# The scan step of a hybrid decoder trunk: conv taps between the chained states, y's low part a step later, the next states' load behind the sample update

## The chip, the cores and the metric

One core of one Trainium2 chip runs the whole kernel. The metric is the device time of one execution in microseconds (us); the time before is the median of three runs.

## What is computed

One inference step of a 2-layer trunk over T = 336 tokens: 64 sample tokens (8 running sequences of 8 steps), 16 meta tokens and 256 prompt tokens. Each layer is a SwiGLU FFN, a mixer and a second FFN. The part of the mixer that the change touches is the Mamba-2 scan. Cut to what matters:

```python
xbc = silu(depthwise_causal_conv(concat([conv0, xbc]), conv_w, conv_b))   # CONV_K = 4 taps
xs, bm, cm = split(xbc)                       # 32 heads of 64 channels, 4 groups, 128 states
dt = softplus(dt_raw + dt_bias)
# ssd_scan, chunk by chunk
lmat = exp(where(causal, seg, -inf))
cb = einsum('bcign,bcjgn->bcijg', cc, bc)
y_intra = einsum('bcijgr,bcjgrp->bcigrp', cb * lmat, xdt)
cs = einsum('bcjgn,bcjgrp->bcgrpn', bc, xdt * decay_end)
final, prev = scan(lambda s, c: (s * decay + cs, s))          # chained states
y_inter = einsum('bcign,bcgrpn->bcigrp', cc, prev) * exp(acum)
y = y_intra + y_inter + d_skip * xs
y = rmsnorm(y * silu(z), ssd_norm)
ssd_out = y @ w_ssd_branch
```

The new states (`final`) of the prompt and of each sample sequence are outputs too.

## The kernel before

Channels lie on the 128 partitions, tokens along the free dimension. Every product of an activation with a weight is made in three matmuls, high part times high part, low times high, high times low (`unit`, L1012). A weight unit is 8 tiles of 128 x 128: SyncE loads it (`wraw`), ScalarE makes its high part (`whi`, L429), GpSimd its low part (`wlo`, L354), two units ahead of their use.

The scan of a layer has 16 steps, one for each 128 channels (2 heads), four steps to a group. On TensorE, ScalarE and GpSimd the first three groups are a hardware loop over groups with four steps written out in its body, and the last group is unrolled behind it; so it is on VectorE too. No scheduler orders anything: each engine runs its own program, in the order written, and semaphores join them. A wait holds up everything behind it on its engine.

Step t on **TensorE** (`ssd_step`, L1121): the xBC unit of tile t+1 into bank 1; the chunk states (L1135, into `kb[3]`); the intra products (L1143, into `kb[0]`); `log_l` of t+1; the z unit of tile t into bank 0, with the products of the sample states in between (L1157, into `kb[1]`); the inter-chunk products of the prompt (L1164, `y_full`); the sample update (L1173, `su_full`); then, behind a wait for `y_read`, the token-major transposes of tile t+1 (`x_token_major`, L1118), which overwrite `kb[0]`.

Step t on **VectorE** (`ssd_step`, L782): the whole conv of tile t+1 (L735 to L747: history, entry, four taps with a drain between any two); behind the chunk states and behind the store of the last step's states (`so_free`), a copy (L789) and the chaining of the states (L794, `p_done`); `times_l` of t+1 (L770); the z bank times 1/rms (L809); y: times its decay (L813), plus D times x (L815), plus the intra part (L817, `y_read`), times the gate (L820, `val_in`); `times_dt` of t+1 (L779, L780); the sample states plus their update (L828, `so_done`); last the sum of squares (L832) and the low part of y (L833, `b_done`), which reads the z bank once more. TensorE's next z unit waits for `b_done`.

Step t on **ScalarE** (`ssd_step`, L511): a weight split, the exponentials of L, the conv rows' store and the SiLU of the conv (`silu_xbc`, L495, L496); a second split; the SiLU of z (L521); behind `val_in` the high part of y (L523) and its square (L524); the load of the next sample states (L534, behind GpSimd's `st_dec`); `head_rows` (two activations, L501); and, behind `so_done`, the store of the new states (L531), whose landing raises `so_free`.

GpSimd decays the sample states into the output tile `so` (L391) behind `so_free` and the load. `so` is one tile: decay, chaining and sample adds of a step write it, and the store reads it.

Of the kernel before, what the change touches and what calls it, by code (L numbers as in the profile page):

```python
# [19 lines left out]
F32 = mybir.dt.float32  # L20
# [6 lines left out]
CONV_K, MAX_WIN = 4, 16  # L27
# [25 lines left out]
G_SSD = 6 * KD  # L53
# [95 lines left out]
def build(nc, x_in, wts, par_in, con_in, own_dram, cst_in, pst_in, ssm_in, y_out, ssm_out, conv_out, pool_out):  # L149
    with ExitStack() as ctx:  # L150
# [153 lines left out]
        p_done = sem("states_chained")  # L304
        y_full = sem("y_products_ready")
# [111 lines left out]
        def _(act):  # L417
# [93 lines left out]
            def ssd_step(L, t, q, rows, last):  # L511
# [9 lines left out]
                act.activation(zb, zb, ACT.Silu).then_inc(gate_done, 1)  # L521
                act.wait_ge(val_in, L * N_VAL + V_Y + t + 1)
                act.activation(bhi[:, t, :], zb, ACT.Copy, scale=par[:, L, bass.ds(G_SSD + t, 1)]).then_inc(hi_done, 1)  # L523
                act.activation(sq[:, 0, :], zb, ACT.Square).then_inc(sq_done, 1)  # L524
                if not last:
                    act.wait_ge(st_dec, L * KI + t + 1)
                    load_states(L, t + 1)
# [123 lines left out]
        def _(dve):  # L651
# [76 lines left out]
            def conv(L, c, m, bank, pair, side):  # L728
# [12 lines left out]
                dve.drain()  # L741
                n = CW - HIST
                cv = gb[bank][:, 0:n]
                dve.tensor_scalar(cv, xp[:, 0:n], pcol(L, G_CW + CONV_K * c), None, ALU.mult)
                for k in range(1, CONV_K):
                    dve.drain()
                    ins = dve.scalar_tensor_tensor(cv, xp[:, k:k + n], pcol(L, G_CW + CONV_K * c + k), cv, ALU.mult, ALU.add)  # L747
                ins.then_inc(cv_in, 1)
# [33 lines left out]
            def ssd_step(L, t, j, g, g_next, pair, last):  # L782
                kt, q = L * KI + t, j % 2
                if not last:
                    conv(L, 2 * N_GROUPS + t + 1, M0["ssd"] + 2 * t + 1, XS_BANK, pair, 1 - q)
# [5 lines left out]
                for c, dst in ((1, pst[:, 1, :]), (2, so[:, SEQS * P:SO])):  # L791
                    for h in range(2):
# [5 lines left out]
                ins.then_inc(p_done, 1)  # L798
                if j == TILES_PER_GROUP - 1 and not last:
                    group_b(g_next)  # L800
# [10 lines left out]
                dve.wait_ge(e_exp, kt + 1)  # L811
                dve.wait_ge(y_full, kt + 1)
                dve.tensor_tensor(yi, yi, eab[:, q, :], ALU.mult)  # L813
                dve.drain()
                dve.scalar_tensor_tensor(t_a[:, 0, :], xs[:, q, :], pcol(L, G_D + t), yi, ALU.mult, ALU.add)  # L815
                dve.drain()
                dve.tensor_tensor(t_a[:, 1, :], kb[0][:, 0:T], t_a[:, 0, :], ALU.add).then_inc(y_read, 1)  # L817
                dve.drain()
                dve.wait_ge(gate_done, L * N_GATE + KF + t + 1)
                dve.tensor_tensor(zb, zb, t_a[:, 1, :], ALU.mult).then_inc(val_in, 1)  # L820
                if not last:
                    times_dt(L, t + 1)

                dve.wait_ge(st_dec, kt + 1)
                dve.wait_ge(su_full, kt + 1)
                for b in range(2):
# [3 lines left out]
                dve.wait_ge(hi_done, L * N_HI + H_Y + t + 1)  # L830
                dve.wait_ge(sq_done, L * N_SQ + S_Y + t + 1)
                dve.tensor_tensor(acc[:, :], acc[:, :], sq[:, 0, :], ALU.add)  # L832
                dve.scalar_tensor_tensor(blo[:, t, :], zb, pcol(L, G_SSD + t), bhi[:, t, :].bitcast(F32),  # L833
                                         ALU.mult, ALU.subtract).then_inc(b_done, 1)
                dve.drain()

            for L in range(DEPTH):
# [81 lines left out]
                with dve.Fori(0, N_GROUPS - 1) as g:  # L919
                    for j in range(per):  # L920
                        ssd_step(L, per * g + j, j, g, g + (j + 1) // per, per // 2 * g + N_GROUPS + (j + 1) // 2, False)
                for j in range(per):
                    ssd_step(L, KI - per + j, j, N_GROUPS - 1, N_GROUPS - 1, (KI - per) // 2 + N_GROUPS + (j + 1) // 2, j == per - 1)
# [493 lines left out]
```

## Time and profile before

| | |
|---|---|
| median of 3 runs | 2165.03 us (2163.43 to 2165.84) |
| the profiled execution's own time | 2164.07 us |
| its span | 2162.3 us |
| TensorE busy (matmul) | 2008.5 us, 93% |
| VectorE busy | 966.3 us, 45% |
| ScalarE busy | 925.6 us, 43% |
| GpSimd busy | 1246.0 us, 58% |
| chain that ended last | TensorE 84%, VectorE 9% |

The two scans lie at about 353 to 592 us and 1412 to 1662 us of the span. Durations are read from the profiled execution. Its time is the span and 1.8 us around it, and it lies 1 us below the median. In the views, PE is TensorE, PEld its weight loads, DVE VectorE, ACT ScalarE, POOL GpSimd; ACTq is ScalarE's sequencer, where DMAs are issued. A row of the timeline with x3 gives the time from the first's start to the third's end. "[0.98 <-DVE t_a L817]" is idle time before the instruction and what ended it; "issue" is time in which the engine waited for nothing that the profile shows.

### The profile page before, as it was taken

Reading aid. Unit: us, or ns where it says so; the run is one execution under the profiler, and the core shown is the slowest. Engines: PE = TensorE matmul, PEld = TensorE weight load, DVE = VectorE, ACT = ScalarE, POOL = GpSimd, SP = SyncE. Lnnn points to the kernel's source line nnn. Section 1 sums busy time; section 2 is a strip of 40 time slices with the busy share of each in tenths; the row PEclk is TensorE's granted clock in tenths of the full one; section 3 lists DMA queues with packets and bytes.
Section 4 is the critical chain, followed back from the end, with each engine's and each line's share of the span. In section 5 each row is a group of like instructions: output and inputs, shape, how many; then the busy total and the mean of one; then the engine's idle time right before and its main releaser. Section 6 shows DMA issues by size and latency. Waiting matters only on the chain.

```text
span 2162.3 us, 39577 instructions
## 1 busy us (share of the span) xinstructions
PE 2008.5 (93%) x13486; PEld 1972.4 (91%) x13486; DVE 966.3 (45%) x2021; ACT 925.6 (43%) x1354; POOL 1246.0 (58%) x555
## 2 busy tenths in 40 slices
PE   6999978999999997999999998789998999899997
PEld 6999977889899997999889998788888999889997
DVE  3221177777645425221152212777776363352212
ACT  4343355555333434333343333455554234443332
POOL 5667743444366565666666666434444666666675
PEclk9999998999899999999999999999999999999998
DMA  4444422444344443444434444234344444434442
GB/s 162 145 142 155 156 80 91 153 141 151 125 153 145 145 138 97 141 141 155 146 99 144 151 154 138 80 102 152 131 152 143 134 147 136 138 101 141 145 156 103
DMA packets 86328, 292.28 MB, mean 135 GB/s; under 512 B 15728, under 2 KB 15728, under 8 KB 86256
## 3 DMA queue, kind: packets, MB, share of 16 engines
q1 hardware_dynamic: 68544, 249.13, 35.8%
q10 hardware_dynamic: 17712, 42.22, 5.6%
q8 instruction: 42, 0.69, 0.1%
q14 instruction: 30, 0.25, 0.0%
HBM read 269.29 MB, written 22.02 MB: 135 GB/s over the span
## 4 chain that ended last, share of the span: by engine, by line
PE 84%; DVE 9%; DVEq 2%; issue 2%; DMA 1%; ACT 1%; POOL 1%; ACTq 0%; SPq 0%
PE gb L1021 25%; PE gb L1025 23%; PE gb L1024 23%; PE kb L1157 1%; PE gb L1073 1%; DVE gb L747 1%; PE gb L1076 1%; PE gb L1077 1%; DVEq L701 1%; PE kb L1143 1%; PE kb L1135 1%; DVE t_a L696 1%; DVE t_a L815 1%; PE kb L1118 1%; PE kb L1164 1%
## 5 line engine op out<-in xcount | busy, mean ns | idle before, releaser
L354 POOL TENSOR_TENSOR wlo<-wraw,whi 128x1024 fp32r<-128x1024 f32 x474 | 1139.5, 2404 | 829.7 <-ACT whi L429 811.9
L1021 PE MATMUL gb<-ahi,whi 128*128 128x336 f32 x2256 | 745.6, 331 | 21.3 <-ACT bc L496 6.3
L1025 PE MATMUL gb<-ahi,wlo 128*128 128x336 f32 x2256 | 721.7, 320 | 0.0
L1024 PE MATMUL gb<-alo,whi 128*128 128x336 f32 x2256 | 720.6, 319 | 0.0
L429 ACT ACTIVATE whi<-wraw 128x1024 fp32r<-128x1024 f32 x474 | 494.7, 1052 | 183.7 <-PE gb L1021 122.6
L1021 PEld LDWEIGHTS gb<-ahi,whi 128*128 128x128 f32 x2256 | 431.3, 191 | 27.8 <-POOL wlo L354 11.0
L1024 PEld LDWEIGHTS gb<-alo,whi 128*128 128x128 f32 x2256 | 431.6, 191 | 0.0
L1025 PEld LDWEIGHTS gb<-ahi,wlo 128*128 128x128 f32 x2256 | 429.4, 190 | 0.0
L1021 PE MATMUL gb<-bhi,whi 128*128 128x336 f32 x1248 | 395.6, 317 | 4.4 <-DVE blo L975 4.4
L1024 PE MATMUL gb<-blo,whi 128*128 128x336 f32 x1248 | 393.6, 315 | 0.0
L1025 PE MATMUL gb<-bhi,wlo 128*128 128x336 f32 x1248 | 393.2, 315 | 0.0
L710 DVE TENSOR_TENSOR t_a<-gb,rpre 128x336 f32<-128x336 f32 x176 | 88.6, 507 | 341.1 <-PE gb L1025 340.1
L1021 PEld LDWEIGHTS gb<-bhi,whi 128*128 128x128 f32 x1248 | 235.1, 188 | 5.0 <-DVE blo L975 5.0
L1024 PEld LDWEIGHTS gb<-blo,whi 128*128 128x128 f32 x1248 | 235.5, 189 | 0.0
L1025 PEld LDWEIGHTS gb<-bhi,wlo 128*128 128x128 f32 x1248 | 235.1, 188 | 0.0
L723 DVE COPY fo<-gb 128x336 f32 x48 | 24.4, 508 | 294.3 <-PE gb L1025 294.3
L473 ACT ACTIVATE bhi<-t_b 128x336 f32 (+1 forms) x88 | 42.7, 485 | 247.6 <-DVE t_b L713 247.6
L486 ACT ACTIVATE sq<-fo 128x336 f32 x48 | 23.3, 486 | 224.9 <-DVE fo L723 224.9
L1073 PE MATMUL gb<-ahi,whi 128*128 128x336 f32 x192 | 68.9, 359 | 42.8 <-DVE alo L688 39.3
L469 ACT ACTIVATE t_b<-t_a 128x336 f32<-128x336 f32 x88 | 42.7, 486 | 124.3 <-DVE t_a L710 124.3
L747 DVE SCALAR_TENSOR_TENSOR gb<-xp,par,gb 128x360 f32<-128x360 f32 x144 | 86.0, 597 | 17.9 <-issue 12.5
L1157 PEld LDWEIGHTS kb<-bc,st 128*128 128x128 f32 x512 | 90.4, 194 | 0.0
(169 smaller groups left out, 2080.6 us busy)
## 6 DMA issues: line engine op xcount, KB each, us to landing
wraw<-wts SPq DMA_DIRECT2D x474, 512.0 KB, 3.7
ssm_o<-tail ACTq DMA_DIRECT2D x32, 576.0 KB, 4.0
st<-ssm_in ACTq DMA_DIRECT2D x32, 512.0 KB, 4.6
x<-x_in ACTq DMA_DIRECT2D x2, 672.0 KB, 5.0
y<-x ACTq DMA_DIRECT2D x2, 672.0 KB, 3.2
pool_o<-tail ACTq DMA_DIRECT2D x2, 540.0 KB, 5.3
tail<-pst_in ACTq DMA_DIRECT2D x2, 480.0 KB, 4.3
conv_o<-cso ACTq DMA_DIRECT2D x48, 13.5 KB, 2.0
```

What stands on the lines that cost most here:

```text
L354: pool.tensor_tensor(wlo[:, s, :], wraw[:, s, :], whi[:, s, :].bitcast(F32), ALU.subtract).then_inc(w_lo, 1)
L429: act.activation(whi[:, slot, :], wraw[:, slot, :], ACT.Copy).then_inc(w_hi, 1)
L469: act.activation(t_b[:, 2 * q, :], t_a[:, 2 * q, :], ACT.Silu).then_inc(gate_done, 1)
L473: act.activation(bhi[:, 2 * i + q, :], t_b[:, 2 * q + 1, :], ACT.Copy).then_inc(hi_done, 1)
L710: dve.tensor_tensor(t_a[:, r, :], gb[r][:, 0:T], rpre[:, :], ALU.mult).then_inc(g_out, 1)
L723: dve.tensor_copy(fo[:, RING * i + j, :], gb[j][:, 0:T]).then_inc(g_out, 1)
L747: ins = dve.scalar_tensor_tensor(cv, xp[:, k:k + n], pcol(L, G_CW + CONV_K * c + k), cv, ALU.mult, ALU.add)
L1021: ins = pe.matmul(gb[bank][:, 0:T], whi[:, slot, w], xh, start=first and j == 0, stop=False)
L1024: pe.matmul(gb[bank][:, 0:T], whi[:, slot, w], xl, start=False, stop=False)
L1025: ins = pe.matmul(gb[bank][:, 0:T], wlo[:, slot, w], xh, start=False, stop=last and j == tiles - 1)
L1073: ins = pe.matmul(gb[s][:, 0:T], whi[:, s, w], ahi[:, j, :], start=j == 0, stop=False)
L1157: pe.matmul(kb[1][:, c], st[:, b * P:(b + 1) * P], bc[:, cg, c], start=True, stop=True)
```

## The change

- **VectorE.** The conv is cut in two: `conv_entry` (up to the filled `xp`) and `tap(k)`. The entry and tap 0 stay in front. Then comes the low part of the *last* step (`low_part(t - 1)`: sum of squares and `blo`), then the copy and the chained states, with tap 1 ahead of the first pair and tap 2 ahead of the second. Behind them D times x plus the intra part, straight from `kb[0]` (`t_a[:, 0]`), raises `y_read`, behind a wait on a new semaphore `yi_full`; then tap 3. The sample adds (`so_done`) move up behind the z bank's scaling, then `times_dt`, and y comes last: times its decay, plus `t_a[:, 0]`, times the gate. The drains between the taps and the one at the end of the step are gone. The first group is peeled from the loop, since its first step has no low part to make; after the last step one more `low_part` is called.
- **TensorE.** The intra products raise `yi_full`; the inter-chunk products (`y_full`) stand last in the step, behind the transposes. The wait for `p_done` stays ahead of the sample update.
- **ScalarE.** The load of the next states moves ahead of the wait for `val_in` and waits for `su_full` too. The store of the new states stays where it was, behind `head_rows`.

```diff
@@ ScalarE, ssd_step
                 act.activation(zb, zb, ACT.Silu).then_inc(gate_done, 1)
+                if not last:
+                    act.wait_ge(st_dec, L * KI + t + 1)
+                    act.wait_ge(su_full, L * KI + t + 1)
+                    load_states(L, t + 1)
                 act.wait_ge(val_in, L * N_VAL + V_Y + t + 1)
...
-                if not last:
-                    act.wait_ge(st_dec, L * KI + t + 1)
-                    load_states(L, t + 1)
                 if rows:
                     head_rows(L, t + 2)
@@ VectorE
+            def low_part(L, t):
+
+                zb = gb[Z_BANK][:, 0:T]
+                dve.wait_ge(hi_done, L * N_HI + H_Y + t + 1)
+                dve.wait_ge(sq_done, L * N_SQ + S_Y + t + 1)
+                dve.tensor_tensor(acc[:, :], acc[:, :], sq[:, 0, :], ALU.add)
+                dve.scalar_tensor_tensor(blo[:, t, :], zb, pcol(L, G_SSD + t), bhi[:, t, :].bitcast(F32),
+                                         ALU.mult, ALU.subtract).then_inc(b_done, 1)
...
-                    conv(L, 2 * N_GROUPS + t + 1, M0["ssd"] + 2 * t + 1, XS_BANK, pair, 1 - q)
+                    conv_entry(L, nxt, M0["ssd"] + 2 * t + 1, XS_BANK, pair, 1 - q)
+                    tap(L, nxt, XS_BANK, 0)
+                if not first:
+                    low_part(L, t - 1)
 
                 dve.wait_ge(cs_full, kt + 1)
                 dve.wait_ge(so_free, 16 * kt + 16)
                 dve.tensor_copy(pst[:, 0, :], kb[3][:, 0:P])
                 dve.drain()
                 for c, dst in ((1, pst[:, 1, :]), (2, so[:, SEQS * P:SO])):
+                    if not last:
+                        tap(L, nxt, XS_BANK, c)
                     for h in range(2):
...
                 ins.then_inc(p_done, 1)
+                dve.wait_ge(yi_full, kt + 1)
+                dve.scalar_tensor_tensor(t_a[:, 0, :], xs[:, q, :], pcol(L, G_D + t), kb[0][:, 0:T], ALU.mult, ALU.add).then_inc(y_read, 1)
+                dve.drain()
+                if not last:
+                    tap(L, nxt, XS_BANK, CONV_K - 1)
...
-                with dve.Fori(0, N_GROUPS - 1) as g:
+                for j in range(per):
+                    ssd_step(L, j, j, 0, (j + 1) // per, N_GROUPS + (j + 1) // 2, j == 0, False)
+                with dve.Fori(1, N_GROUPS - 1) as g:
...
+                low_part(L, KI - 1)
@@ TensorE, ssd_step
                 pe.wait_ge(p_done, kt + 1)
-                for c in (1, 2):
-                    c0, n = CHUNKS[c]
-                    ins = pe.matmul(kb[1][:, c0:c0 + n], pst[:, c - 1, :], bc[:, cg, c0:c0 + n], start=True, stop=True)
-                ins.then_inc(y_full, 1)
...
                     x_token_major(L, t + 1, 1 - q)
+                for c in (1, 2):
+                    c0, n = CHUNKS[c]
+                    ins = pe.matmul(kb[1][:, c0:c0 + n], pst[:, c - 1, :], bc[:, cg, c0:c0 + n], start=True, stop=True)
+                ins.then_inc(y_full, 1)
```

VectorE, the front of a step of the last group (unrolled in both kernels), before: `gb` is a PSUM bank, here the conv's; `fo` holds the chained states; `tail_50` the output tile of the states; the semaphore `new_states_stored` is `so_free`, `chunk_states_ready` is `cs_full`.

```order
L744 TENSOR_SCALAR gb<-xp,par 128x360
L747 SCALAR_TENSOR_TENSOR gb<-xp,par,gb 128x360 x3
L789 COPY fo<-kb 128x128 [waits new_states_stored,chunk_states_ready]
L794 SCALAR_TENSOR_TENSOR fo<-fo,dec,kb 128x64 x2
L794 SCALAR_TENSOR_TENSOR tail_50<-fo,dec,kb 128x64 x2
```

And now (lines are those of the changed kernel):

```order
L751 TENSOR_SCALAR gb<-xp,par 128x360
L802 TENSOR_TENSOR acc<-acc,sq 128x336 [waits square_ready,hi_part_ready]
L803 SCALAR_TENSOR_TENSOR blo<-gb,par,bhi 128x336
L817 COPY fo<-kb 128x128 [waits new_states_stored,chunk_states_ready]
L753 SCALAR_TENSOR_TENSOR gb<-xp,par,gb 128x360
L824 SCALAR_TENSOR_TENSOR fo<-fo,dec,kb 128x64 x2
L753 SCALAR_TENSOR_TENSOR gb<-xp,par,gb 128x360
L824 SCALAR_TENSOR_TENSOR tail_50<-fo,dec,kb 128x64 x2
L830 SCALAR_TENSOR_TENSOR t_a<-t_b,par,kb 128x336 [waits intra_products_ready]
L755 SCALAR_TENSOR_TENSOR gb<-xp,par,gb 128x360
```

Three of the four taps have moved behind the copy and its two waits, the low part has moved in ahead of it, and the product with D stands among them.

VectorE, the back of a step of the last group, from the z bank's scaling on, before: `kb` in L813 holds the inter-chunk products, `t_a` the sum of y, `tail_50` in L779 and L780 the dt products.

```order
L809 TENSOR_TENSOR gb<-gb,rpre 128x336 [waits gemm_bank_full]
L813 TENSOR_TENSOR kb<-kb,eab 128x336 [waits y_products_ready,decay_per_channel_ready]
L815 SCALAR_TENSOR_TENSOR t_a<-t_b,par,kb 128x336
L817 TENSOR_TENSOR t_a<-kb,t_a 128x336
L820 TENSOR_TENSOR gb<-gb,t_a 128x336 [waits gate_ready]
L779 TENSOR_TENSOR tail_50<-kb,tail_50 128x384 [waits x_transposed]
L780 TENSOR_TENSOR tail_50<-kb,tail_49 128x384
L828 TENSOR_TENSOR tail_50<-tail_50,kb 128x512 [waits sample_update_ready,states_decayed]
```

And now:

```order
L844 TENSOR_TENSOR gb<-gb,rpre 128x336 [waits gemm_bank_full]
L850 TENSOR_TENSOR tail_50<-tail_50,kb 128x512 [waits sample_update_ready,states_decayed]
L850 TENSOR_TENSOR tail_50<-tail_50,kb 128x512
L794 TENSOR_TENSOR tail_50<-kb,tail_50 128x384 [waits x_transposed]
L795 TENSOR_TENSOR tail_50<-kb,tail_49 128x384
L857 TENSOR_TENSOR kb<-kb,eab 128x336 [waits y_products_ready,decay_per_channel_ready]
L859 TENSOR_TENSOR t_a<-kb,t_a 128x336
L862 TENSOR_TENSOR gb<-gb,t_a 128x336 [waits gate_ready]
```

The sample adds and the dt products now stand ahead of y, whose last product (L862, `val_in`) is the last of the step.

ScalarE, the end of a step of the last group, before: `value_ready` is `val_in`, `new_states_ready` is `so_done`, `tail_50` the output tile of the states.

```order
L521 ACTIVATE gb<-gb 128x336 [waits gemm_bank_evicted]
L523 ACTIVATE bhi<-gb,par 128x336 [waits value_ready]
L524 ACTIVATE sq<-gb 128x336
L534 DMA st<-ssm_in 128x1024 [waits states_decayed]
L501 ACTIVATE rx<-ss,con 128x336 x2
L531 DMA ssm_o<-tail_50 128x1152 [waits new_states_ready]
```

And now:

```order
L522 ACTIVATE gb<-gb 128x336 [waits gemm_bank_evicted]
L536 DMA st<-ssm_in 128x1024 [waits sample_update_ready,states_decayed]
L528 ACTIVATE bhi<-gb,par 128x336 [waits value_ready]
L529 ACTIVATE sq<-gb 128x336
L502 ACTIVATE rx<-ss,con 128x336 x2
L533 DMA ssm_o<-tail_50 128x1152 [waits new_states_ready]
```

The load has moved ahead of the wait for `value_ready`; the store has not moved.

## Rows read from the trace of the kernel before

**Rows 1.** All waits of the run: who waited for whom, us in total, times, longest.

```profile
PE kb L1118 <- DVE t_a L817: 28.8, 30, 1.2
```

**Rows 2.** The chain that ended last, 480 to 520 us: start us, us, what.

```profile
483.85 0.54 PE kb L1118 x3
...
488.14 0.67 PE kb L1135 x6
...
490.70 0.15 PE gb L1021
...
496.10 0.56 PE kb L1164 x4
...
497.44 0.56 DVE t_a L815
498.08 0.52 DVE t_a L817
...
498.72 0.54 PE kb L1118 x3
```

**Rows 3.** Timeline of TensorE in that step: start us, us, engine, line, operation.

```profile
496.58 1.16 PE L1173 MATMUL kb<-tail,fo 32*128 32x128 f32 x16
```

**Rows 4.** Timeline of VectorE, a step inside the loop of layer 1.

```profile
478.85 1.21 DVE L758 TENSOR_TENSOR fo<-tail,con 64x1024 f32<-64x1024 f32 x1
...
489.42 0.60 DVE L744 TENSOR_SCALAR gb<-xp,par 128x360 f32<-128x360 f32 x1 [0.20 <-issue]
...
491.73 0.60 DVE L747 SCALAR_TENSOR_TENSOR gb<-xp,par,gb 128x360 f32<-128x360 f32 x1 [0.17 <-issue]
492.24 0.28 DVE L789 COPY fo<-kb 128x128 f32<-128x128 f32 x1
492.69 0.47 DVE L794 SCALAR_TENSOR_TENSOR fo<-fo,dec,kb 128x64 f32<-128x64 f32 x2 [0.17 <-issue]
493.33 0.47 DVE L794 SCALAR_TENSOR_TENSOR tail<-fo,dec,kb 128x64 f32<-128x64 f32 x2 [0.17 <-issue]
...
499.43 0.56 DVE L779 TENSOR_TENSOR tail<-kb,tail 128x384 f32<-128x384 f32 x1 [0.15 <-PE kb L1118]
...
500.37 1.27 DVE L828 TENSOR_TENSOR tail<-tail,kb 128x512 f32<-128x512 f32 x2
501.56 0.50 DVE L832 TENSOR_TENSOR acc<-acc,sq 128x336 f32<-128x336 f32 x1
501.98 0.56 DVE L833 SCALAR_TENSOR_TENSOR blo<-gb,par,bhi 128x336 f32 x1
```

**Rows 5.** Timeline of VectorE, two steps of the unrolled last group.

```profile
549.01 1.94 DVE L747 SCALAR_TENSOR_TENSOR gb<-xp,par,gb 128x360 f32<-128x360 f32 x3
...
563.65 1.94 DVE L747 SCALAR_TENSOR_TENSOR gb<-xp,par,gb 128x360 f32<-128x360 f32 x3
```

**Rows 6.** The states' store (L531): who waited for it (us, times), and its landing.

```profile
  DVE fo L789: 7.4, 4
...
DMA to landing us min/median/max: 3.0/4.0/5.9
```

**Rows 7.** Timeline of ScalarE and its sequencer, the same step of the loop.

```profile
490.96 0.34 ACTq L492 DMA_DIRECT2D conv_o<-cso  x1
...
491.57 0.30 ACT L509 ACTIVATE gb<-gb 80x160 f32<-80x160 f32 x1
...
493.95 0.48 ACT L496 ACTIVATE t_b<-gb,par 128x272 f32<-128x272 f32 x1
...
499.44 0.54 ACT L523 ACTIVATE bhi<-gb,par 128x336 f32 x1 [2.43 <-DVE gb L820]
...
501.80 0.34 ACTq L531 DMA_DIRECT2D ssm_o<-tail  x1
```

**Rows 8.** Busy time by stretch: us, each engine's busy us, granted clock, DMA share, GB/s.

```profile
577.00:583.00 6.00, 6.00 (x31) 5.67 (x31) 1.24 (x5) 0.00 (x0) 3.53 (x2) 0.50 0.13 52
1470.00:1485.00 15.00, 13.81 (x103) 12.98 (x101) 10.89 (x24) 6.86 (x12) 7.29 (x4) 0.89 0.44 150
```

## Prediction before the run

> **What bounds the kernel now.** I first read the page's busy shares: TensorE is busy for 93% of the span, so only a stage in which it stands idle can give much back. The view of all waits names such a stage: 30 times TensorE stands before the three token-major transposes of a scan step (L1118) until VectorE has read the last step's products (L817), 28.8 us in all [rows 1]. The 30 are the 15 steps of each layer that have a successor.
>
> Next I read the chain of waits for one step [rows 2]. From one group of transposes to the next it is 14.87 us (498.72 - 483.85). Weights and products run back to back from 484.39 to 496.66 (496.10 + 0.56). The chain then leaves TensorE for VectorE: L815, L817, and only then L1118. TensorE itself still has the 16 sample-update matmuls there, until 497.74 (496.58 + 1.16) [rows 3], and then idles 0.98 us. So a step is TensorE's work of 13.89 us plus that wait. The work is: transposes 0.54, xBC unit 3.75 (484.39 to 488.14), states, intra products and log L 2.56, z unit 5.40, y products 0.56, sample update 1.08 (497.74 - 496.66).
>
> Third, VectorE's own timeline [rows 4]: in the loop an operation behind a drain starts about 0.1 us later than it does in the last group of four, which is unrolled: from the first tap to the last it is 2.31 us for three, or 0.77 each, against 1.94 - 0.60 = 1.34 for two, or 0.67 each [rows 4, 5]. There a step takes 14.64 us (563.65 - 549.01) [rows 5].
>
> Last, the DMA that stores the new states (L531): it lands 3.0 to 5.9 us after its issue, 4.0 in the median, and VectorE's copy L789 waited for it only 4 times [rows 6]. It is nearly harmless now, and I believe that it decides after the change.
>
> **The change, part by part.**
>
> *The wait of TensorE.* y_read now comes from the product of D and the intra part, which VectorE does before the z unit is over, and the inter-chunk products move behind the transposes. That takes the 0.98 us off 30 steps: at most 29 us.
>
> *The low part a step later.* It stands behind the next step's conv entry and first tap. TensorE's z unit waits for it, since it reads the z bank. From the end of the xBC unit: 1.28 us to the first tap (488.14 to 489.42), 0.51 for a tap without a drain behind it (491.73 to 492.24), 0.42 for the sum, 0.56 for the difference, 0.12 to reach TensorE (498.08 + 0.52 to 498.72): 2.89 us [rows 2, 4]. TensorE's own work in that stretch is 2.56, so a wait of 0.3 us is new. TensorE's path is then about 13.9 to 14.2 us a step; the low end because the 0.54 of the transposes is a price after a wait.
>
> *Taps between the chained states.* The same instructions, with four drains fewer in all (three between taps, one at the end of the step). But three of the four taps now stand behind the copy that waits for the stored states; before, all four stood ahead of it.
>
> *The store of the states.* Its data are ready earlier, since the sample update is now added ahead of the dt products. Its issue is not: on ScalarE's queue it still stands behind the wait for the gated y (L523), and that value is now the last thing VectorE does in a step. So a loop closes: store issued, landed, copy, taps, SiLU, transposes, dt products, y, ScalarE, next store. Its terms:
> - landing 4.0, and 0.17 until the waiter starts, as from L1118's end (498.72 + 0.54) to L779 (499.43) [rows 2, 4, 6];
> - copy 0.45, tap 0.51, two state products and their drain 0.64, tap 0.51, two products 0.47, the D product and its drain 0.64 (497.44 to 498.08), last tap 0.60: 3.82 [rows 2, 4];
> - tap's end (491.73 + 0.60) to the end of the SiLU (493.95 + 0.48): 2.10 [rows 4, 7];
> - 0.12 to TensorE, transposes 0.54, 0.17 back, dt products 0.94 (499.43 to 500.37): 1.77 [rows 2, 4];
> - three operations of y with two drains, 0.64 + 0.64 + 0.52: 1.80 [rows 2];
> - value to the store's issue: 0.15 to ScalarE and 0.35 for the sequencer: 0.5.
>
> Sum 14.16 us. In the first step of a group the product L758 (1.21 us) stands ahead of the sample adds [rows 4] and in the last step two copies do; spread over four steps that, with landings that scatter, costs about 0.3: **14.5 us in the loop**. Without the loop's five 0.1 us it is about 14.1 in the unrolled groups, of which there are now two per layer, the first having been peeled on VectorE.
>
> The 0.35 is the weakest term but the landing. Four activations now stand ahead of the store on ScalarE (L523, L524, two of L501). The DMA of conv rows is a like case with three: it was issued at 490.96, 0.61 us before the third of them started [rows 7]. So the sequencer runs ahead; the bounds are 0.2 and, if it could run only two ahead, 1.3 (0.2 and two activations like L523 with 0.54 and L496 with 0.48). I take 0.35, near that row. The Trainium skill (Advanced Engine Details and Errata, Engine Queue Depths) gives ScalarE a queue of 8: by it four fit, and the sum stays as it is. With a queue that held fewer it would be up to 0.9 longer, and the step no faster than now. No run here shows four waiting.
>
> *The next states' load* is issued behind the sample update, some 2 us earlier in the step. It was waited for nowhere; it stays at nothing. What it does is to part two transfers: the load used to go out right behind L523's start (499.44), 2.4 us ahead of the store (501.80) [rows 7], and now goes out about 3 us ahead of L523 and so some 3.5 us ahead of the store.
>
> *The last step of a layer.* TensorE waits there for the so adds; now it waits for the dt products and then, with no conv work between, for the low part. The first is shorter, the second new; I take nothing. After that idling the clock was at 0.50, its lower level of 1.2 GHz, in layer 1 [rows 8], and I expect it again.
>
> **The sum.** 16 loop steps gain 14.87 - 14.5 = 0.37: 5.9 us. Eight steps of the first groups gain 14.87 - 14.1 = 0.77: 6.2. Six of the last groups gain 14.64 - 14.1 = 0.54: 3.2. Together 15.3 us. In layer 2 the granted clock of four stretches of 15 us, one of them in [rows 8], is 0.89 where the others in the loop show 1.00: 0.11 x 15 = 1.65 us each, 6.6 in all. Layer 1 had the same waits and shows none, so what sets it off is not sure. The wait that comes back is shorter and in two pieces, so I take 4.5 of it. 19.8 us off the profiled execution's 2164.07 is 2144.3; the median of the runs is 1 us above that execution, so **2145 us**.
>
> **Rivals.**
> *TensorE bounds it (the store lands sooner).* The store ran beside the states' load and will run more apart from it; its shortest landing is 3.0 [rows 6]. From about 3.7 down the loop is under TensorE's path: 14.1 in the loop, 14.0 or so elsewhere. 24 x 0.8 + 6 x 0.55 = 22.5, plus 6.6 of clock: 29 us off, 2136. All 29 us of waits, the 6.6 and 3 us for the clock in one last step would be 2126, the low end. For it: half the landings are under 4.0. Against: the store will start close behind a load of weights. The Trainium skill (DMA: Bandwidth & Descriptors, Latency and other measured facts) says that a transfer's fixed cost is smaller under lighter HBM load, which speaks for this rival; the spread of 3.0 to 5.9 agrees with that.
>
> *The store becomes the bound for the worse.* If it lands in 5.0 us, between median and maximum, as beside the weights it may, every step of the loop is 15.5, and 15.1 in the unrolled groups: 16 x 0.6 + 8 x 0.25 + 6 x 0.45 = 14 us more, with no clock won: about 2180. It decides from a landing of 4.5, where 15.3 / 30 = 0.5 us a step is eaten. The same follows from an issue 0.8 us later. For it: the wait is moved ahead of three taps, the SiLU and the transposes. Against: a median of 4.0 with a load beside it already.
>
> *It evens out.* Landing near 4.5: TensorE's wait moves from y_read to the SiLU'd xBC tile, of the same length: 2160 to 2168.
>
> **How the numbers follow.** Forecast 0.50, TensorE-bound 0.24, even 0.12, slower 0.14. Even is within 0.2%, or 4.3 us, about what this kernel's measurement can tell from no change. So faster 0.74, same 0.12, slower 0.14. The range runs from 2126 to 2170: below is nothing priced, above the worse part of the slower case, about 0.1. The forecast's own range is 2136 to 2156.
>
> **What would show it.** After: no wait of L1118's successor on y_read; instead the transposes wait for ScalarE's SiLU, 0.2 to 0.6 us a step, and the z unit up to 0.3 us for the low part; VectorE's copy waits for the store in most steps, about 1 us; loop steps of 14.3 to 14.7 us and shorter ones in the first group; fewer stretches of layer 2 under 1.00. It is wrong if the copy waits for nothing and steps take under 14.1, or if the transposes wait 1 us or more for the xBC tile.

## The result, and the profile after the change

| kernel | median, us | runs | range, us |
|---|---|---|---|
| before | 2163.98 | 8 | 2160.13 to 2165.84 |
| changed | 2184.61 | 8 | 2174.12 to 2216.20 |

The change made the kernel slower: ratio 1.0093, 95% interval 1.0072 to 1.0114 (two disturbed runs, of 2207.6 and 2216.2 us, are left out of it; the median of the other six is 2181.1). I had predicted 2145 us, with a range up to 2170. The profiled execution took 2182.81 us, with a span of 2181.0.

First the page: busy time by engine, and the chain that ended last.

```profile
PE 2030.7 (93%) x13486; PEld 1993.3 (91%) x13486; DVE 961.8 (44%) x2021; ACT 919.8 (42%) x1354; POOL 1246.3 (57%) x555
...
PE 80%; DVE 9%; DVEq 3%; DMA 3%; issue 3%; ACT 1%; POOL 1%; ACTq 0%; SPq 0%
```

TensorE has the same 13486 matmuls and is busy 22 us longer than before (2008.5), so part of them ran at the lower clock; and DMA is now 3% of the chain, where it was 1%. Next all waits: who waited for whom, us in total, times, longest.

```profile
DVE fo L817 <- DMA ssm_o<-tail: 34.1, 23, 3.4
...
PE gb L1051 <- DVE blo L803: 24.8, 18, 4.1
...
POOL tail L392 <- DMA ssm_o<-tail: 21.3, 11, 6.4
...
PE kb L1148 <- ACT t_b L497: 6.4, 8, 1.4
```

The wait of the transposes for y [rows 1] is gone, as it should be. Two waits stand in its place. VectorE's copy L817 (L789 before, 7.4 us [rows 6]) waits 34.1 us for the states' store, and the z unit on TensorE (L1051) waits 24.8 us for the low part, up to 4.1 us at a time, where I had allowed 0.3. The store's own landing:

```profile
DMA to landing us min/median/max: 2.7/4.1/5.8
```

Nearly the 3.0, 4.0 and 5.9 of before [rows 6]. So the store did not become slow; VectorE came to wait for it.

Now one bad step of layer 1. VectorE's timeline, the front of the step, then GpSimd's and TensorE's at the same time:

```profile
457.59 0.60 DVE L751 TENSOR_SCALAR gb<-xp,par 128x360 f32<-128x360 f32 x1 [0.21 <-issue]
458.09 2.58 DVE L802 TENSOR_TENSOR acc<-acc,sq 128x336 f32<-128x336 f32 x1
460.60 0.55 DVE L803 SCALAR_TENSOR_TENSOR blo<-gb,par,bhi 128x336 f32 x1
461.38 0.29 DVE L817 COPY fo<-kb 128x128 f32<-128x128 f32 x1 [0.23 <-DMA ssm_o<-tail]
```

```profile
457.94 2.37 POOL L355 TENSOR_TENSOR wlo<-wraw,whi 128x1024 fp32r<-128x1024 f32 x1 [2.97 <-ACT whi L430]
```

```profile
461.38 0.42 PE L1051 MATMUL gb<-ahi,whi 128*128 128x336 f32 x1 [2.51 <-DVE blo L803]
```

The sum of squares L802 took 0.50 us before [rows 4], and does so here too in most steps (500 ns in the median). Here it takes 2.58. GpSimd's low weight split L355 began 0.15 us ahead of it and ended at 460.31; the sum ends 0.36 us after that, so it stood for nearly all of the split and then ran. Nine of its 32 instances take 1.29 to 2.68 us; eight of them end 0.36 us after a split, and one (2.05 us, at 1486.67) 0.36 us after the decay L392, GpSimd's other product of that size. L803, the low part's difference, has one of its inputs in PSUM, the matmuls' output memory, and is never longer than 0.56. The Trainium skill (SBUF — State Buffer, Who interferes with whom) says that a VectorE instruction with two SBUF inputs contends with a GpSimd instruction that reads SBUF, and that the later one blocks until the first is done; the trace agrees. The clock by stretches of 15 us (engines' busy us, granted clock, DMA share, GB/s):

```profile
440.00:455.00 15.00, 14.01 (x115) 13.23 (x114) 11.11 (x29) 8.42 (x14) 6.67 (x3) 1.00 0.42 146
455.00:470.00 15.00, 12.49 (x75) 11.93 (x73) 9.01 (x21) 8.07 (x13) 5.95 (x3) 0.76 0.37 110
470.00:485.00 15.00, 13.77 (x92) 12.97 (x91) 9.40 (x24) 5.59 (x10) 4.98 (x3) 0.78 0.45 145
```

After these 2.51 us of idling the granted clock of the two stretches is 0.76 and 0.78 where it was 1.00, so part of them ran at 1.2 GHz, the lower of the two levels; from this step's store to the next it is 21.3 us (455.56 to 476.90). Such steps exist in both layers, with clocks down to 0.59 in layer 2 (1560 to 1575 us).

To compare kernels I use **the length of a step**: the time from a layer's first issue of the states' store to its fifteenth, by 14. Before that is 14.86 us in layer 1 (367.26 to 575.27) and 15.30 in layer 2 (1433.28 to 1647.49, with its stretches at a lower clock); after, 15.37 and 16.39. (15.37 + 16.39 - 14.86 - 15.30) x 14 = 22 us: the whole loss lies in these steps (the two profiled executions, of 2182.81 and 2164.07 us, are 19 us apart).

### The profile page after: what moved, and what is told of

Same layout as the page of the kernel before. It is cut to its first block, busy times and chain, and to the rows that moved or that the text cites. A ratio compares the mean times of both kernels' runs of the same rounds, so it can differ in the third digit from the quotient of the medians.

```text
span 2181.0 us, 39321 instructions
## 1 busy us (share of the span) xinstructions
PE 2030.7 (93%) x13486; PEld 1993.3 (91%) x13486; DVE 961.8 (44%) x2021; ACT 919.8 (42%) x1354; POOL 1246.3 (57%) x555
## 4 chain that ended last, share of the span: by engine, by line
PE 80%; DVE 9%; DVEq 3%; DMA 3%; issue 3%; ACT 1%; POOL 1%; ACTq 0%; SPq 0%
PE gb L1051 24%; PE gb L1054 23%; PE gb L1055 23%; DMA ssm_o<-tail 2%; PE kb L1199 1%; PE gb L1103 1%; PE kb L1188 1%; PE gb L1106 1%; PE gb L1107 1%; DVE gb L753 1%; DVEq L703 1%; DVE t_a L698 1%; POOL wlo L355 1%; DVE xp L737 1%; PE kb L1206 1%
## 5 line engine op out<-in xcount | busy, mean ns | idle before, releaser
L355 POOL TENSOR_TENSOR wlo<-wraw,whi 128x1024 fp32r<-128x1024 f32 x474 | 1139.6, 2404 | 851.5 <-ACT whi L430 832.8
L1051 PE MATMUL gb<-ahi,whi 128*128 128x336 f32 x2256 | 754.6, 334 | 45.7 <-DVE blo L803 24.8
L1051 PEld LDWEIGHTS gb<-ahi,whi 128*128 128x128 f32 x2256 | 435.7, 193 | 57.2 <-issue 30.6
L1051 PE MATMUL gb<-bhi,whi 128*128 128x336 f32 x1248 | 394.7, 316 | 4.4 <-DVE blo L1005 4.4
L1051 PEld LDWEIGHTS gb<-bhi,whi 128*128 128x128 f32 x1248 | 234.3, 188 | 5.0 <-DVE blo L1005 5.0
L1103 PE MATMUL gb<-ahi,whi 128*128 128x336 f32 x192 | 68.8, 358 | 40.7 <-DVE alo L690 37.3
L1188 PEld LDWEIGHTS kb<-bc,st 128*128 128x128 f32 x512 | 97.1, 208 | 0.0
```

Of the source, the lines that this page charges most:

```text
L355: pool.tensor_tensor(wlo[:, s, :], wraw[:, s, :], whi[:, s, :].bitcast(F32), ALU.subtract).then_inc(w_lo, 1)
L1051: ins = pe.matmul(gb[bank][:, 0:T], whi[:, slot, w], xh, start=first and j == 0, stop=False)
L1103: ins = pe.matmul(gb[s][:, 0:T], whi[:, s, w], ahi[:, j, :], start=j == 0, stop=False)
L1188: pe.matmul(kb[1][:, c], st[:, b * P:(b + 1) * P], bc[:, cg, c], start=True, stop=True)
```

## Experiments

Each experiment was timed in five rounds with the kernel before on the same chip (2160.6 to 2161.9 us there); the changed kernel's row is that of the result above (2163.98 us for the kernel before). "Taps back" means the three taps, as they were before the change, ahead of the copy. Differences in the text are of medians; taken from the ratios to the kernel before, those against the changed kernel differ by up to 4 us.

| kernel | median, us | to before, 95% | step, layer 1 / 2, us | copy waits for store, us |
|---|---|---|---|---|
| changed | 2184.61 | 1.0072 to 1.0114 | 15.37 / 16.39 | 34.1 |
| 1 sum late | 2164.75 | 1.0004 to 1.0028 | 15.02 / 15.11 | 45.1 |
| 2 GpSimd's split later | 2168.64 | 1.0015 to 1.0040 | 15.35 / 15.22 | 47.8 |
| 3 store early | 2138.47 | 0.9876 to 0.9908 | 14.16 / 14.18 | 9.7 |
| 4 sum late, store early | 2131.13 | 0.9839 to 0.9867 | 13.97 / 14.02 | 15.6 |
| 5 taps back | 2135.91 | 0.9855 to 0.9891 | 14.13 / 14.15 | 1.8 |
| 6 low part back | 2159.79 | 0.9979 to 1.0000 | 15.16 / 15.03 | 36.8 |
| 7 load back | 2298.21 | 1.0598 to 1.0673 | 19.72 / 18.71 | 67.9 |
| 8 before, taps moved alone | 2182.52 | 1.0096 to 1.0132 | 15.41 / 15.79 | 43.9 |
| 9 store early, low part exchanged | 2137.79 | 0.9865 to 0.9904 | 14.16 / 14.34 | 9.6 |
| 10 the same, signal on the difference | 2127.96 | 0.9828 to 0.9858 | 13.89 / 13.87 | 10.7 |
| 11 taps back, sum behind the adds | 2133.95 | 0.9865 to 0.9899 | 14.12 / 14.15 | 2.6 |
| 12 taps and low part back | 2133.60 | 0.9857 to 0.9887 | 14.24 / 14.26 | 2.5 |

The first four runs stood between two theories: P, the meeting of the sum with GpSimd's split; and S, the store's loop of the prediction. After them S became V, with VectorE's string in it.

### 1 and 2: the sum of squares, and GpSimd's split

```diff
@@ 1: low_part, then ssd_step on VectorE
-                dve.tensor_tensor(acc[:, :], acc[:, :], sq[:, 0, :], ALU.add)
...
                 if not last:
                     times_l(L, t + 1, g_next)
+                if not first:
+                    square_sum()
```

> The changed kernel with one instruction moved: the sum of squares of the low part goes from ahead of the difference to behind the masked products, so that the z unit no longer waits for it. Theory P (GpSimd): the sum was held up to 2.7 us by GpSimd's weight split and made the z unit, then the clock, late; out of that path, TensorE's waits for the difference fall from 24.8 us to under 8, the stretches at half speed in layer 1 go (now 0.76 to 0.78 at 455 to 485 us), and the time falls from 2184.6 us to 2145 to 2165. Theory S (store): a step is long because the store of the states lands up to 5.8 us after its issue and the copy waits for it; the move gains under 10 us, and the copy's waits for the store stay near 34 us or grow.

```diff
@@ 2: ssd_step on ScalarE
-                    ahead(L, "ssd", 1 + 2 * q, 2 * t - 2 * q)
                     exp_l(L, t + 1, 1 - q)
+                    ahead(L, "ssd", 1 + 2 * q, 2 * t - 2 * q)
```

> The changed kernel with ScalarE's first weight split of a step moved behind the three exponentials: GpSimd's low split, which follows it, starts some 2.5 to 3 us later, and no instruction of VectorE moves. Theory P: the sum of squares then never runs beside GpSimd's split, takes 0.50 us in every step, TensorE's waits for the difference fall under 8 us, and the time falls to 2145 to 2165. Theory S: no gain of over 10 us, as the store's issue and landing are untouched; the split's 1.05 us even lies on ScalarE ahead of the SiLU of the next step's channels and can delay the transposes.

Both gained: 19.9 us and 16.0 us against the changed kernel (17 and 14 us by the ratios). In the second no VectorE instruction moved, and every sum took 496 to 509 ns; TensorE's waits for the difference fell from 24.8 to 8.9 us (1.6 in the first). So the meeting with GpSimd is shown, and its price is 14 to 20 us. But neither came under the kernel before, and the copy's waits for the store rose to 45.1 and 47.8 us: S held too. With the sum no longer holding the front, the store simply became the later of the two.

### 3 and 4: the store early

```diff
@@ ssd_step on ScalarE
+                act.wait_ge(so_done, L * KI + t + 2)
+                act.dma_start(ssm_out[L * KI + t, :, :], so).then_inc(so_free, 16)
                 act.wait_ge(val_in, L * N_VAL + V_Y + t + 1)
...
-                act.wait_ge(so_done, L * KI + t + 2)
-                act.dma_start(ssm_out[L * KI + t, :, :], so).then_inc(so_free, 16)
```

> The changed kernel with the store of the states issued ahead of the wait for the gated values on ScalarE, instead of behind the two evictions: its issue comes 2 to 3 us earlier. Theory S: the copy's waits for the store (34.1 us in 23 steps) go to under 5 us, steps are bound by TensorE, 2130 to 2150 us. Theory P: the waits for the store go as well, but the sum of squares still meets GpSimd's split (1.3 to 2.7 us where it does) and TensorE still waits 15 us or more for the difference; 2160 to 2185 us, unless the steps' phase moves so that they do not meet.

> The sum of squares late and the store early, both. Either theory alone leaves one of the two moves without effect: by P the time is that of the late sum alone within 5 us, by S that of the early store alone within 5 us. If each is a limit of its own, this is 10 us or more under both, near 2135 us (30 steps of 13.9 us of TensorE's work in place of 14.87 from 2164).

The early store took 46 us off the changed kernel, though it lands no sooner (2.7, 4.7 and 7.0 us): what counts is that it is issued earlier. Its sums are all 0.50 us: in all but one step of each layer GpSimd's split starts 0.5 to 0.9 us after the sum, and with a nearly constant step it stays there. So in this order P follows from the store's loop and is not a limit of its own beside it. The margin is small: in experiment 9 the sum stands 0.5 us later, and one of its 32 takes 2.54 us. The late sum on top (experiment 4) brought 7 us more, where S had said 5 at most: TensorE's 5.4 us of waits for the difference went with it, but for 3.1 us in two waits. The late sum itself met the split in some steps (up to 2.72 us), but nobody on TensorE waits for it there.

### 5 and 8: the taps

```diff
@@ 5: ssd_step on VectorE
                 if not first:
                     low_part(L, t - 1)
+                if not last:
+                    for k in range(1, CONV_K):
+                        dve.drain()
+                        tap(L, nxt, XS_BANK, k)
...
-                    if not last:
-                        tap(L, nxt, XS_BANK, c)
...
-                if not last:
-                    tap(L, nxt, XS_BANK, CONV_K - 1)
```

> The changed kernel with the other three taps back ahead of the copy of the chunk states (behind the low part, with a drain between them), where they can run while the store lands. Theory V (the store's loop as the late sum's run shows it: VectorE's own string from the copy to the gated product, 10.0 us at 458.29 to 468.29, then 0.6 to the store's issue and 4.5 to the next copy, 15.1 in all): 1.8 us of taps leave that string, the loop takes 13.3 us and no longer sets a step; the copy's waits for the store fall from 34.1 us to under 15, and the time to 2135 to 2160. Theory P (GpSimd alone): the sum of squares stands as before ahead of the z unit, its long cases and the waits for the difference stay at 20 to 25 us, and the time stays at 2175 to 2190.

Theory V held, at the low end: 2135.9 us, 49 us under the changed kernel, with everything else of the change in place. The copy's wait is gone, and the store lands like this:

```profile
DMA to landing us min/median/max: 2.7/2.8/4.1
```

It lands sooner, and a likely reason is that it now always starts at the same point between two weight loads; a constant step alone is not enough, since experiment 3 has one too. The DMA view of the changed kernel shows what the store meets elsewhere. From the issue to the landing at 365.85, q10 being ScalarE's queue and q1 that of the weights (packets, MB, share of the 16 engines):

```profile
q10 hardware_dynamic: 144, 0.59, 50.2%
q1 hardware_dynamic: 35, 0.09, 8.3%
...
ssm_o<-tail ACTq DMA_DIRECT2D x1, 576.0 KB, 2.8
```

and at 393.89:

```profile
q1 hardware_dynamic: 144, 0.52, 36.9%
q10 hardware_dynamic: 288, 0.60, 27.5%
...
ssm_o<-tail ACTq DMA_DIRECT2D x1, 576.0 KB, 5.6
```

A landing of 2.8 has next to no weights beside it, one of 5.6 a whole unit. Counted over all stores of the changed kernel, from the packets that start between issue and landing, those of 2.7 and 2.8 us have at most 0.09 MB of weights beside them and those over 5.5 us 0.52 MB each. In the kernel before it is 0.11 MB at most; there the store's scatter of 3.0 to 5.9 us arose beside the states' load. I did not move the weight loads to prove it.

Experiment 8 made the same edit in the other direction: the kernel before, with three taps put behind the copy (two between the chained states, one behind them) and nothing else.

> The kernel before with one part of the change alone: three of the four taps behind the copy of the chunk states, two of them between the chained states and one behind them. Theory V (the taps cost because they stand in the store's loop, and that loop is long only where the store's issue stands behind the last thing VectorE does): in the kernel before the string ends with the sample adds, the loop is about 13.7 us with the taps in it, and TensorE's 14.87 us a step still sets the time: within 8 us of 2162. If taps behind the copy are dear by themselves (they delay the SiLU and the transposes): 30 steps of up to 1.8 us, 2180 to 2215.

This expectation fell: 2182.5 us, as slow as the changed kernel. The copy waits 43.9 us, 24 times, where it waited 7.4:

```profile
  POOL tail L391: 45.5, 25
  DVE fo L804: 43.9, 24
...
DMA to landing us min/median/max: 3.0/4.5/6.6
```

while the transposes wait only 7.4 us for the SiLU. So the taps cost by the store's loop there as well and not by a late SiLU; what was wrong in V is the slack that I gave the kernel before. In layer 1 of the kernel before, inside the loop, the copy mostly starts 5.2 to 5.7 us after the store's issue, and the store has landed after 3.2 to 4.5: that is some 1 to 2 us of cover, and the three taps take 1.6. From the copy to the next issue of the store it is 9.6 to 11.1 us in this run's steps of layer 1 (all but the last) and from the issue to the copy 3.7 to 6.6, together 14.4 to 16.8, where I had put 13.7. In that kernel every sum took 0.50 us, so the sum has no part in its 22 us. On TensorE they appear as clock: it is busy 2031.5 us, 23 more than in the kernel before.

### 6 and 7: the low part, and the load

```diff
@@ 6: ssd_step on VectorE
-                if not first:
-                    low_part(L, t - 1)
...
                 dve.tensor_tensor(zb, zb, t_a[:, 1, :], ALU.mult).then_inc(val_in, 1)
+                low_part(L, t)
+                dve.drain()
@@ 7: ssd_step on ScalarE
-                if not last:
-                    act.wait_ge(st_dec, L * KI + t + 1)
-                    act.wait_ge(su_full, L * KI + t + 1)
-                    load_states(L, t + 1)
...
                 act.activation(sq[:, 0, :], zb, ACT.Square).then_inc(sq_done, 1)
+                if not last:
+                    act.wait_ge(st_dec, L * KI + t + 1)
+                    act.wait_ge(su_full, L * KI + t + 1)
+                    load_states(L, t + 1)
```

> The changed kernel with the low part (sum of squares and difference) back at the end of its own step, so of the two things the change does to it, none. Theory P: TensorE's waits for the difference (24.8 us) and the long sums go; VectorE does the low part while the store lands, which costs nothing; 2150 to 2165 us, as with the late sum (2164.8) or a little less. Theory V: the store's loop of 15.1 us a step stays and holds the time at 2155 to 2170; it can fall below only if the string from the copy on gets shorter, and it does not.

> The changed kernel with the load of the next states back behind the two evictions on ScalarE, just ahead of the store. If the load's place matters, it does so either by GpSimd's decay (which then waits for the load, 2.5 to 4 us later than now, and makes the added states late) or by the store, which would queue behind the load: then 2190 to 2220 us. Theories P and V both say it does not: within 10 us of 2184.6, with the store's landing at its 2.7, 4.1 and 5.8 us.

Experiment 6 came out as P and V both say, and so does not choose between them: sums of 0.51 us, the copy's wait at 36.8, 2159.8 us. Experiment 7 went far past every expectation, to 2298 us. With y last in the step, a load behind its value comes too late: TensorE's z unit, which holds the products from the loaded states, waits for it. The store, now issued right behind the load, lands in 5.3 us in the median, against 4.1, and the copy and GpSimd's decay wait longer for it.

```profile
DVE fo L817 <- DMA ssm_o<-tail: 67.9, 20, 5.8
...
POOL tail L392 <- DMA ssm_o<-tail: 58.4, 29, 9.5
...
PE gb L1051 <- DMA st<-ssm_in: 35.4, 12, 5.4
```

From 365 to 590 us the granted clock is 0.78 there. The load's move is thus no ornament: given the new order on VectorE, it is worth 114 us. How that divides between the late load and the late store is not shown.

### 9 and 10: the order within the low part

```diff
@@ 10: low_part with the early store (9 has the same order, but .then_inc(b_done, 1) on the sum)
-                dve.tensor_tensor(acc[:, :], acc[:, :], sq[:, 0, :], ALU.add)
                 dve.scalar_tensor_tensor(blo[:, t, :], zb, pcol(L, G_SSD + t), bhi[:, t, :].bitcast(F32),
                                          ALU.mult, ALU.subtract).then_inc(b_done, 1)
+                dve.tensor_tensor(acc[:, :], acc[:, :], sq[:, 0, :], ALU.add)
```

> The early store, and the low part's two instructions exchanged: the difference first, which frees the z unit, then the sum, before the copy. Theory V and P together: the store sets no step, the z unit waits 0.5 us less for the difference than with the early store alone (5.4 us there) and the sum runs while TensorE is fed: 2128 to 2136 us, as the early store with the late sum (2131.1), and without that kernel's sums of 1.8 to 2.7 us. If the order of the two does not matter: 2138 us, as the early store alone.

Experiment 9 did not test what its expectation says: I had left the signal on the second of the two, so the z unit waited for both, and 2137.8 equals the early store alone. With the signal moved:

> The early store, and the low part with the difference first, now with the signal to TensorE on the difference and the sum behind it (in the run before, the signal stayed with the sum, so the z unit waited for both in either order). If the wait of 5.4 us counts: 2128 to 2134 us. If not, 2138 as before. By theory P the sum, 0.4 us later than in the early store's run, can meet GpSimd's split at its start: a few sums over 1 us would then show, on VectorE alone and not on TensorE.

2127.96 us, 10 us under experiment 9 and **1.6% under the kernel before**: the lowest median of all, with an interval that overlaps that of experiment 4. No wait of TensorE for the low part is left, no sum was held by the split, and a step is 13.89 and 13.87 us.

### 11 and 12: what else the low part is worth

```diff
@@ 11, with the taps back and the sum out of low_part
                 ins.then_inc(so_done, 1)
+                if not first:
+                    square_sum()
                 if not last:
                     times_dt(L, t + 1)
```

> The taps back ahead of the copy as in the run that gave 2135.9, and the sum of squares moved behind the sample adds, where it meets neither of GpSimd's splits and no engine waits for it. Theories V and P together: the store sets no step, the z unit's 5.9 us of waits for the difference go, a step is TensorE's 13.9 to 14.1 us in place of 14.3 to 14.4: 2123 to 2131 us. If the z unit's wait is only another name for time that TensorE loses anyway: 2133 to 2138.

> The taps back ahead of the copy, and the low part back at the end of its own step as well; left of the change are the early product of D, the order of the sample adds, dt and y, and the load's place. If the low part's move is worth something once the store sets no step: slower than 2135.9 by over 5 us, as VectorE then stands 1 us for ScalarE's evictions and takes the xBC tile 2 us later. If not: 2125 to 2137.

Experiment 11 came out at 2133.95, where the other reading had it, but for another reason. The wait for the difference is gone, and a new one stands there. TensorE's log L waits for the selected head rows (L502), which come behind the evictions of y on ScalarE:

```profile
PE gb L1144 <- ACT rx L502: 19.5, 28, 5.6
```

Without the sum there, in experiment 5, that wait is 11.3 us, 2 times: the 0.4 us that VectorE does ahead of y in each step came back as 8 us in all. Experiment 12 (2133.60, against 2135.91 in experiment 5, with overlapping intervals) says that with the taps back the low part's move, as the change makes it, brings nothing that can be measured.

## Why the prediction was wrong, step by step

**The wait of TensorE and its 13.89 us: right.** The transposes wait for y no more. Experiment 10 has steps of 13.89 and 13.87 us in the mean. That the two agree to the hundredth is luck: single steps there run from 13.38 to 14.47.

**The low part a step later: the wait was right where nothing interferes, the sum's price was wrong.** I worked out 0.3 us of new wait. Experiments 3 and 5 show it, 5.4 us in 15 waits and 5.9 in 16, and a step of 14.13 to 14.18, 0.26 or so above experiment 10. But I priced the sum at 0.42 from a place where GpSimd's split did not run [rows 4], and did not ask what runs beside it in its new place. There it took up to 2.68 us, TensorE idled up to 4.1, and the clock fell. Price: 14 to 20 us (experiments 1 and 2).

**The store's loop: the mechanism and its fixed part were right; the landing was not.** The copy waits for the store in most steps, as I had said. Without the landing my terms sum to 14.16 - 4.17 = 9.99 us. From copy to next issue the trace after has 9.90 us (383.99 to 393.89) and 9.95 (445.61 to 455.56) in steps where nothing else intervened, and 9.7 to 10.6 in the nine steps of layer 1, its last left out, whose copy waited 0.8 us or more. The failed step is "landing 4.0 ... in the loop 14.5": one median for a quantity that goes through 2.8, 4.0 and 5.6 in three successive steps (issues at 365.85, 379.85 and 393.89). A step is the longer of this loop and TensorE's 14 us, so a landing of 2.8 gives nothing back, while 5.6 makes 15.9 us (393.89 to 409.76). "Landings that scatter" stood in the text with 0.3 us for it and the group extras together, and that the store would start close behind a load of weights stood there only as an argument against a rival. With the sum out of TensorE's way (experiment 1) a step is 15.02 and 15.11, against 14.31 on average in my sum (eight of 14.5, seven of 14.1): 0.75 x 28 = 21 us. That and the 20 us of the sum make the 40 us between 2145 and 2184.6. Of the 0.75 the scatter is shown to make about a third: the longer of 14.0 and 9.95 us plus the landing, worked out for each landing of experiment 1, is 14.4 us in the mean of layer 1 and 14.7 in layer 2, an estimate from that trace. Another part lies between the end of the SiLU and that of the dt products, 1.8 to 3.3 us in the same run (2.4 in the mean of the loop's sixteen steps) where I had put 1.77; and four late sums were still held, for up to 2.73 us. What each of these costs was not taken apart.

**The two are one chain.** A loop longer than TensorE's work shifts the store, the gated y and ScalarE's queue against each other from step to step. So sum and split drift over each other, TensorE idles, the clock falls. Experiments 3 and 5, whose steps are nearly constant (13.3 to 14.5 us), show no long sum; that the drift is the reason is read from the timelines, and no run changed the drift alone.

**Taps between the chained states: costed at nothing but their place in the loop.** That place is the loss: ahead of the copy they run while the store lands, behind it they lengthen the loop by the 1.6 us (0.51 + 0.51 + 0.60) that stand in my sum. Experiments 5 and 8 show it from both sides, 49 us off and 22 us on; in the first the sum's price, the clock and the sooner landing went with it.

**The store's issue: right.** The 0.35 us for the sequencer with four activations ahead held: in experiment 1 y ends at 468.29 (467.77 + 0.52) and the store is issued at 468.90, 0.61 us later, against the 0.5 that I had put down for both terms. In the unrolled last group of the changed kernel it is issued at 553.37, 0.04 us after y's end (552.81 + 0.52), when the first of the four activations had just started (553.36). The queue of 8 that the Trainium skill gives ScalarE (Advanced Engine Details and Errata, Engine Queue Depths) agrees with that, as would any that holds four.

**The load: right in time, wrong in rank.** It costs nothing in its new place, but I did not see that the change would not bear its old one.

**The clock: wrong sign.** I had 4.5 us back in layer 2; TensorE was busy 22 us longer instead, over a span that is 19 us longer. So the new waits did not lengthen its idle time in total (154 us before, 150 after): the loss shows as matmuls run at the lower clock. In experiments 3 and 5 its busy time is back at 2008.7 and 2008.8 us and its idle time down to 128 us, so about half of what they gain on the changed kernel is clock.

**The rivals.** The slower one gave 2180 with a landing of 5.0 in every step. Its time was met, its condition was not: the median landed in 4.1. The landings of layer 1's first 15 stores are 4.2 us in the mean, but from issue to copy it was 4.5, since after a long sum VectorE came to the copy later than the store. That it meets the 4.5 from which I had said that the landing decides is chance. The rest was the sum and the clock, which no rival held.

## What to carry to other kernels

Work that is free while a transfer lands is dear behind the wait for it: before moving an instruction past a wait, ask whether the wait was its cover. Price a loop with the spread of its transfer, not the median, since the long landings count and the short ones do not. And price a moved VectorE instruction that reads two SBUF tiles by what GpSimd does at the same moment in its new place.

## What was new about the hardware

VectorE's hold behind GpSimd is not confined to instructions with two inputs. In experiment 8 the copy of the conv history, 0.18 us elsewhere and with one input, ends with GpSimd's split to 0.03 us, one of seven such copies in that run (1.05 to 1.55 us):

```profile
460.19 1.11 DVE L735 COPY xp<-cst 128x24 f32 x1 [2.25 <-PE gb L1045]
```

```profile
458.90 2.37 POOL L354 TENSOR_TENSOR wlo<-wraw,whi 128x1024 fp32r<-128x1024 f32 x1 [2.39 <-ACT whi L429]
```

In the changed kernel it happened once, in its longest step (25.1 us, from the store at 1480.54 to the next), with TensorE's longest wait, 4.1 us: the copy was held by the split, and then the sum by the decay.

```profile
1483.04 2.29 DVE L737 COPY xp<-cst 128x24 f32 x1 [3.12 <-PE gb L1055]
...
1486.67 2.05 DVE L802 TENSOR_TENSOR acc<-acc,sq 128x336 f32<-128x336 f32 x1
```

```profile
1482.92 2.37 POOL L355 TENSOR_TENSOR wlo<-wraw,whi 128x1024 fp32r<-128x1024 f32 x1 [3.07 <-ACT whi L430]
1486.45 1.91 POOL L392 TENSOR_TENSOR tail<-st,dec 128x1024 f32<-128x1024 f32 x1 [1.16 <-DMA ssm_o<-tail]
```

And one store of 576 KB landed in 2.7 to 5.8 us within one kernel, mostly longer the more weights were moved beside it; in experiment 5, with a constant start, the median was 2.8 with not one weight load moved in the program.
